# Decoder step: cache loads under the projection, eight gate chunks in each attention stage, the causal triangle as a product

## What is computed

```
u = rmsnorm(x) * g_mix
z = u @ w_in          # q, k, v of 12 dilated heads; q, k, v of 8 stick-breaking heads; gates ga, gb (1024 each)
x += (sigmoid(ga) * (oa @ w_oa) + sigmoid(gb) * (ob @ w_ob)) @ w_out
```

```
log_1mb = where(j < i, -softplus(s), 0);  suffix = cumsum from the right
a = where(j < i, exp(-softplus(-s) + suffix - log_1mb), 0);  ob = a @ v
```

## Time and profile before

| | |
|---|---|
| Time, median of 3 runs | 2026.39 us (2022.48 to 2026.89) |
| Profiled execution, its own time | 2021.45 us |
| Span of its trace | 2019.8 us |
| TensorE busy | 1746.6 us (86%) |
| VectorE busy | 1197.1 us (59%) |
| ScalarE busy | 962.2 us (48%) |
| Mean DMA rate | 186 GB/s |

### The profile page before, as it was taken

One profiled execution on the slowest core, in us unless ns is written; L12 is line 12 of the kernel. 1 busy time (PEld: TensorE's weight loads), 2 busy tenths in 40 slices (PEclk: granted clock), 3 DMA queues, 4 the chain that ended last, 5 costly groups with the idle time before them and its releaser, 6 DMA issues. The chain is left out here.

```text
span 2019.8 us, 27422 instructions
## 1 busy us (share of the span) xinstructions
PE 1746.6 (86%) x9832; PEld 1491.5 (74%) x9832; DVE 1197.1 (59%) x1564; ACT 962.2 (48%) x1351; POOL 200.5 (10%) x294
## 2 busy tenths in 40 slices
PE   5999999959888887676597973999999999994898
PEld 4999999948666666354496852788888888873785
DVE  5122221125499997432464236899999999993664
ACT  4112111111476775134442112778787878782454
POOL 0011110030000000000130001311111111111000
PEclk7999999979899999675798985999999999997899
DMA  4344443196351200500345314999999999993420
GB/s 126 116 125 126 126 126 105 53 275 215 100 179 53 74 31 19 193 1 12 105 136 180 125 44 147 386 387 385 384 382 383 389 389 384 388 384 125 175 79 32
DMA packets 151862, 375.80 MB, mean 186 GB/s; under 512 B 21507, under 2 KB 94835, under 8 KB 131300
## 3 DMA queue, kind: packets, MB, share of 16 engines
q1 hardware_dynamic: 116594, 308.16, 42.2%
q0 software_dynamic: 15424, 36.00, 5.7%
q10 hardware_dynamic: 19762, 30.56, 4.4%
HBM read 326.86 MB, written 72.12 MB: 198 GB/s over the span
## 5 line engine op out<-in xcount | busy, mean ns | idle before, releaser
L96 PE MATMUL p_acc<-uh,p_wl 128*128 128x344 f32 x720 | 234.9, 326 | 8.5 <-DVE ul L329 8.5
L98 PE MATMUL p_acc<-uh,p_wh 128*128 128x344 f32 x720 | 231.1, 321 | 0.0
L97 PE MATMUL p_acc<-ul,p_wh 128*128 128x344 f32 x720 | 231.1, 321 | 0.0
L306 ACT ACTIVATE p_zc<-p_acc 128x344 f32<-128x344 f32 x90 | 41.2, 457 | 292.4 <-PE p_acc L98 288.1
L2313 DVE TENSOR_TENSOR x_wgl<-x_wg,x_wgh 128x2048 fp32r<-128x2048 f32 x66 | 148.3, 2287 | 16.2 <-ACT x_wgh L2250 14.8
L2313 DVE TENSOR_TENSOR x_wul<-x_wu,x_wuh 128x2048 fp32r<-128x2048 f32 x66 | 148.3, 2288 | 15.9 <-ACT x_wuh L2250 15.8
L2335 DVE TENSOR_TENSOR x_wdl<-u,x_wdh 128x1024 fp32r<-128x1024 f32 x128 | 148.2, 1219 | 11.2 <-ACT x_wdh L2256 11.2
L96 PEld LDWEIGHTS p_acc<-uh,p_wl 128*128 128x128 f32 x720 | 136.0, 189 | 11.9 <-issue 8.2
L342 DVE COPY p_zk<-p_tp 128x512 f32<-128x512 f32 x40 | 25.8, 686 | 193.8 <-PE p_tp L259 193.8
L97 PEld LDWEIGHTS p_acc<-ul,p_wh 128*128 128x128 f32 x720 | 136.2, 189 | 0.0
L98 PEld LDWEIGHTS p_acc<-uh,p_wh 128*128 128x128 f32 x720 | 136.2, 189 | 0.0
(11 more groups left out here) (375 smaller groups left out, 4246.7 us busy)
## 6 DMA issues: line engine op xcount, KB each, us to landing
x_wg<-in_w_gate SPq DMA_DIRECT2D x64, 1024.0 KB, 8.1
x_wu<-in_w_up SPq DMA_DIRECT2D x64, 1024.0 KB, 8.3
u<-in_w_down SPq DMA_DIRECT2D x32, 2048.0 KB, 12.6
zT<-p_zc ACTq DMA_DIRECT2D x30, 516.0 KB, 3.5
p_w<-in_w_in SPq DMA_DIRECT2D x30, 512.0 KB, 5.4
ztok<-p_zk POOLq DMA_DIRECT2D x20, 512.0 KB, 4.7
m_gate<-gT SPq DMA_DIRECT2D x16, 516.0 KB, 4.3
f_y<-ys POOLq DMA_DIRECT2D x16, 512.0 KB, 5.1
```

The source lines that it names most:

```text
L96: pe.matmul(out, w_low, m_high, start=first, stop=False)
L97: pe.matmul(out, w_high, m_low, start=False, stop=False)
L98: return pe.matmul(out, w_high, m_high, start=False, stop=last)
L306: act.activation(zc[:, b, s * NS:(s + 1) * NS], acc[b * NSPLIT + s][:, 0:NS], ACT.Copy).then_inc(zc_full, 1)
```

## The change

Three things are done together.

A class `Ahead` holds the buffers and loads of decode. `project` now issues them from SP between its passes: the window rows of keys and values, the page table, the key pages, then queries, and after the last weights the first two gate chunks. The memsets of K, Q and V move to GpSimd at the start of `project`. The passes are reordered: the five of q first and not kept, the ten of k and v last and kept. Decode itself loads only the own rows of k and v, the value pages and the stick-breaking queries. The key pages now lie where `u` was, and the by-token copies of `project` lie in a spare part of another buffer.

`DECODE_GATES` goes from 6 to 8: decode has 24 groups, stick-breaking 576 gate matmuls in place of 720. The steps of decode move forward.

The triangle is rounded once by ScalarE, and TensorE adds it to the scores of the diagonal block by a product with the identity in rounded fp32. The addition of line 678 is gone.

```diff
-DECODE_GATES = 6
+DECODE_GATES = 8
 # project
-        RUNS = [(0, CA, CA, True), (CA, KEPT, 3 * CA + CB - 2 * CA, True),
-                (KEPT, KEPT + CA // 2, -2 * KEPT, False),
-                (KEPT + CA // 2, PASSES, 3 * CA - 2 * (KEPT + CA // 2), False)]
+        RUNS = [(0, CA // 2, 0, False), (CA // 2, QUERIES, 2 * CA, False),
+                (QUERIES, QUERIES + CA, -CB, True), (QUERIES + CA, PASSES, 0, True)]
...
+            def ahead(n):
+                if n == 0:
+                    a.cached(sp, a.K, 0, 0, a.kq_in)
+                    a.cached(sp, a.V, 1, 0, a.v_in)
+                if n == 1:
+                    sp.wait_ge(cleared, 3)
+                    for x in (1, 2):
+                        a.cached(sp, a.K, 0, x, a.kq_in)
+                        a.cached(sp, a.V, 1, x, a.v_in)
+                    sp.dma_start(a.table[:, :], ...)
+                if n == 2:
+                    sp.wait_ge(ul_full, KD)
+                    sp.wait_ge(a.table_in, 16)
+                    for b in range(DEC // 2):
+                        a.load_page(sp, a.PK, b, 0, a.ek_in[b])
+                if n == 3:
+                    for b in range(DEC // 2, DEC):
+                        a.load_page(sp, a.PK, b, 0, a.ek_in[b])
+                    for b in range(2):
+                        sp.wait_ge(k_out[b], QUERIES * 16)
+                    for x in range(N_DIL):
+                        a.query(sp, x, a.kq_in)
+                        a.own_row(sp, a.Q, 0, x, a.kq_in)
+            each_pass(sp, step, ahead)      # ahead(n) follows the first pass of run n
+            for c in range(2):
+                sp.dma_start(a.gw[c], win_v[:, :, QKV + c * P:QKV + (c + 1) * P]).then_inc(a.gw_in[c], 16)
 # decode_and_gates
-        D_SCORES_T, D_PROBS_T, D_VALUES = 6, 7, 8
-        S_SCORES_T, S_WEIGHTS_T, S_VALUES = 13, 14, 16
-        S_SCORES = {8: (0, 2), 9: (2, 4), 10: (4, 6), 11: (6, 8)}
+        D_SCORES_T, D_PROBS_T, D_VALUES = 4, 5, 6
+        S_SCORES_T, S_WEIGHTS_T, S_VALUES = 10, 11, 13
+        S_SCORES = {4: (0, 2), 5: (2, 4), 6: (4, 6), 7: (6, 8)}
...
-                if n == D_SCORES_T - 3:
+                if n == 0:
                     dilated_scores(0)
                     dilated_scores(1)
 # stick_and_gates, TensorE
+                edge = c * HALF + n == (i + 1) * P
                 for b in range(2):
-                    pe.matmul(S[:, b, 0:n], q..., k..., start=True, stop=True).then_inc(s_full, 1)
+                    last = pe.matmul(S[:, b, 0:n], q..., k..., start=True, stop=not edge, ...)
+                    if edge:
+                        last = pe.matmul(S[:, b, n - P:n], unit_r[:, :], causal[:, :], start=False, stop=True, ...)
+                    last.then_inc(s_full, 1)
 # ScalarE
+            act.activation(unit_r[:, :], ident[:, :], ACT.Copy).then_inc(rounded, 1)
+            act.wait_ge(const, 2)
+            act.activation(causal[:, :], drawn[:, :], ACT.Copy).then_inc(rounded, 1)
 # VectorE
-                    diag = z[:, u % ZB, i * P:(i + 1) * P]
-                    dve.tensor_tensor(diag, diag, causal[:, :], ALU.add).then_inc(masked, 1)
...
-                    dve.wait_ge(masked, u + 1)
+                    dve.wait_ge(z_full, scaled(u) + 1)
```

More of the change, by code:

```diff
@@ L210, in project @@
             "p_uh_full", "p_ul_full"))
+        cleared = sem("p_cleared")
+        a = g["ahead"]
         u, uh, ul, ident, zT, ztok = g["u"], g["uh"], g["ul"], g["ident"], g["zT"], g["ztok"]
@@ L215, in project, with each_pass @@
         PASSES = CHUNKS // 2
-        KEPT = CA + CB
+        QUERIES = (CA + CB) // 2
+        KEPT = PASSES - QUERIES
         GROUPS = [(0, 4), (4, 4)]
-        RUNS = [(0, CA, CA, True), (CA, KEPT, 3 * CA + CB - 2 * CA, True),
-                (KEPT, KEPT + CA // 2, -2 * KEPT, False),
-                (KEPT + CA // 2, PASSES, 3 * CA - 2 * (KEPT + CA // 2), False)]
-        def each_pass(eng, step):
-            for lo, hi, shift, kept in RUNS:
+        RUNS = [(0, CA // 2, 0, False), (CA // 2, QUERIES, 2 * CA, False),
+                (QUERIES, QUERIES + CA, -CB, True), (QUERIES + CA, PASSES, 0, True)]
+        def each_pass(eng, step, between=None):
+            for n, (lo, hi, shift, kept) in enumerate(RUNS):
                 step(lo, shift, kept)
+                if between:
+                    between(n)
                 inner = hi - (hi == PASSES)
@@ L237, in final, with opens @@
             return isinstance(it, int) and it == PASSES - 1
-        def kept_before(it):
-            return isinstance(it, int) and it <= KEPT
+        def opens(it):
+            return isinstance(it, int) and it == QUERIES
         @block.sync
@@ L281, in step @@
                     elif not first(it):
-                        turn(it - 1, 1, kept or kept_before(it))
+                        turn(it - 1, 1, kept and not opens(it))
             each_pass(pe, step)
-            turn(PASSES - 1, 1, False)
+            turn(PASSES - 1, 1, True)
         @block.scalar
@@ L349, in _ @@
         def _(pool):
+            for t in (a.K, a.Q, a.V):
+                pool.memset(t[:, 1, :, :], 0.0).then_inc(cleared, 1)
             def step(it, shift, kept):
@@ L546, in scores @@
                     need(pe, z_full, z_first[st, c] - 1 + b)
-                    pe.matmul(S[:, b, 0:n], q[x][h, i * P:(i + 1) * P], k[x][h, c * HALF:c * HALF + n],
-                              start=True, stop=True).then_inc(s_full, 1)
+                    last = pe.matmul(S[:, b, 0:n], q[x][h, i * P:(i + 1) * P], k[x][h, c * HALF:c * HALF + n],
+                                     start=True, stop=not edge, skip_group_check=True)
+                    if edge:
+                        last = pe.matmul(S[:, b, n - P:n], unit_r[:, :], causal[:, :], start=False, stop=True,
+                                         skip_group_check=True)
+                    last.then_inc(s_full, 1)
             def turn(u):
@@ L1178, in decode_and_gates @@
                 "e_sT_full", "e_z_full", "e_w_full", "e_t_full", "e_al_full", "e_a_full", "e_aT_full",
                 "e_aT_read", "e_oT_full"))
-        ek_in = [sem(f"e_k_in{b}") for b in range(DEC)]
-        gw_in = [sem(f"g_w_in{j}") for j in range(2)]
+        kq_in, v_in, ek_in, gw_in = a.kq_in, a.v_in, a.ek_in, a.gw_in
         g_out = [sem(f"g_g_out{j}") for j in range(2)]
         gwh_full, gwl_full, acc_full, gate_full = map(sem, ("g_wh_full", "g_wl_full", "g_acc_full", "g_gate_full"))
-        pages = g["cache_sb"].rearrange("a n k c h d -> (a n) k c (h d)")
@@ L1233, in _ @@
+            for x in range(N_DIL):
+                a.own_row(sp, K, A_W, x, kq_in)
             for x in range(N_DIL):
[L1234 to L1237 removed]
+                a.own_row(sp, V, 2 * A_W, x, v_in)
             sp.wait_ge(scored, 2)
             for b in range(DEC):
[L1240 to L1241 removed]
+                a.load_page(sp, PV, b, 1, ev_in)
@@ L2719, in build @@
             g["spare_small"] = flat2[:, (CB + 4) * NT:TT * D]
-            before = list(nc.free_semaphores)
-            with nc.sbuf_tensor("u", [P, KD, NT], F32) as g["u"]:
+            opened = ExitStack()
+            ahead_sem = lambda n: ctx.enter_context(nc.semaphore(n))
+            with nc.sbuf_tensor("s_bias0", [P, 2], F32) as bias0, nc.sbuf_tensor("u", [P, KD, NT], F32) as g["u"]:
+                g["ahead"] = Ahead(g, lambda n, s, d=F32: opened.enter_context(nc.sbuf_tensor(n, s, d)), ahead_sem)
+                before = list(nc.free_semaphores)
                 norm_in(nc, g, x_of)
                 project(nc, g)
-            with nc.sbuf_tensor("e_pk", [P, 8 * SEQ], F32) as shared, nc.sbuf_tensor("s_bias0", [P, 2], F32) as bias0:
+                shared = g["u"][:, :, :].rearrange("p k n -> p (k n)")[:, 0:8 * SEQ]
                 part = [shared[:, n * SEQ:(n + 1) * SEQ] for n in range(8)]
```

147 lines of the change are left out of this document (66 added, 81 removed).

## The result

The changed kernel took 2029.09 us, the median of 10 runs (2027.33 to 2034.82), beside 2025.15 (2021.01 to 2027.45) for the kernel before on the same chip: a ratio of 1.0030, 95% interval 1.0018 to 1.0042 (here and below the ratio is estimated over all the runs together; the two medians alone give 1.0019). It is slower by 0.2 to 0.3%. The forecast was 2018.0, faster by 0.4%. The profiled execution's span grew from 2019.8 to 2027.2 us.

The account below looks back on a forecast made before the run. TensorE was taken to bound the projection, loads to cost decode about 13 us, and VectorE to pace stick-breaking. Projection +3.7, decode +6.9 and stick-breaking −19 gave −8.4 us: median 2018.0, range 2008 to 2029.

Parts of the forecast that it names:

- Stick-breaking: the mask: Stick-breaking: VectorE loses 64 additions, −12.8 us, and waits, −1.6; TensorE's 64 added products, 8.3 us, fit its waiting.
- Projection: Projection: the added loads cost TensorE 0 us, bounds 0 and +5.
- End of the projection: Last projection pass, now a kept one: added transposes, copies and stores end the block 3.7 us later, bounds +2 and +6.
- Start of decode: Decode before ScalarE's first cut: gate weights already loaded, so three of four issues and a wait go, −2.4 us.
- The new one before the dilated outputs: Decode step 8: TensorE waits for VectorE's d_own, a new stall of 2.5 us, bounds 0 and 6.
- Two chunks fewer in stick-breaking: Stick-breaking: less gate work gives −2.3 us for VectorE's cuts, −2.9 in the opening, −1.5 in the drain.
- The opening's −2.9: Stick-breaking's opening: the third cut moves to step 4, so the first scan starts earlier, −2.9 us.
- A, the clock: Stick-breaking: TensorE's clock falls in more places, 2 us each; slower from six on, 2034 with eight; chance 0.11.
- three signs that I named as disproof: TensorE waits in projection; stick-breaking's granted clock below 0.95; VectorE's waits for transposes from 6.4 to over 15 us.
- B, the loads: Projection: load bursts delay weights and stall TensorE, +9 us, so 2027; chance 0.05 at twice its price.
- C: Stick-breaking gives only mask and cuts, −14 us, decode's new stall is 6; net 0, 2026; chance 0.22 with other small forms.
- D: All waits go: no new decode stall, projection's end costs 2, stick-breaking gives 25; −18.6 us, 2008; chance 0.19.

Follow-up runs that it names:

- grouped order: The changed kernel with both heads' score products issued first and both triangle products after them; 2016.59 us, ratio 0.9968.
- the pair was split: The kernel before, with one gate product per step from step 8 on moved between both heads' score products, no mask on TensorE; 2032.46 us, ratio 1.0044.

## Why the prediction was wrong

The ratios split the change as the sum did, each times 2022 us. In the sum, loads are +3.7 − 2.4 − 12.9 − 1.2 − 1.7 + 2.5 = −12.0; the two chunks are +22.6 − 2.3 − 2.9 − 1.5 = +15.9; the mask is −12.8 − 1.6 + 0.7 + 1.4 = −12.3.

| part | forecast | measured | from |
|---|---|---|---|
| loads and steps | −12.0 | −11.5 | 0.9943 − 1 |
| two chunks to decode | +15.9 | +19.8 | 1.0041 − 0.9943 |
| mask on TensorE | −12.3 | −2.2 | 1.0030 − 1.0041 |
| sum | −8.4 | +6.1 | 1.0030 − 1 |

The −2.2 of the mask is smaller than the intervals of the two ratios are wide (5 and 6 us), so it can't be told from nothing.

*The step that failed* is in "Stick-breaking: the mask": "I take 0.129, 8.3 us; all of it lies inside TensorE's 39.4 us of waiting for VectorE, and nothing is added." I priced 64 products by their own length and said of their place only that a change of kind might treble it. What counted was what stood on either side: two products that had shared the engine. TensorE's work grew by 34.5 us instead, and the stage came out 1.1 us longer and not 19 shorter. The upper bound, 25 us, was also under the 34.5, because it was a bound on the masks and not on their neighbours. The trace of before showed both heads' 384 keys as one group of four records, 0.85 us, but no head alone to hold it against; the shape in that row, 64*128, and the slices of 64 partitions in the code were what could have made me ask. The Trainium skill ("TensorE: Matmul & The Clock Gate", "The mechanism") says that small products on different row groups of the array overlap, and that a weight load overlaps a running product only where the row groups differ. On the first the traces agree (0.85 us for two heads, 0.84 for one). On the second they don't as it stands: in the projection products and weight loads take all 128 rows, and TensorE is busy 240.00 and its loads 239.19 of the same 240 us. That a product over all rows between the two heads ends their overlap is shown; by what mechanism is not.

With the order mended, the kernel has a ratio of 0.9968; the forecast was 2018.0 / 2026.39 = 0.9959. That they are so near is partly luck: the stage is then 10.1 us shorter, where 19 was forecast. The mask in the grouped order takes 6.4 off it and not 12.3, and what follows the last gate eviction happened to be 3.8 shorter in that profile.

*The terms, one by one.* Projection: right, 240.00 of 240, no wait for weights. End of the projection: +1.9, not +3.7, just under my lower bound of 2. Start of decode: from first issue to first cut 1.74 us (411.73 to 413.47) in place of 4.05, so −2.3, near the −2.4 of the forecast. The stall of 12.9 went. The new one before the dilated outputs is 1.3, not 2.5, yet it costs more than its length: the group around it takes 7.8 us (451.21 to 459.01) and not 3.77, with the clock granted at 0.76 and 0.82 of full, so for part of each at the level of 1.2 and not 2.4 GHz. I had counted a fall behind the old stall and none behind the new. Decode in all: its last eviction is 11.0 later, the sum to that point was +3.7 + 6.9 = +10.6. Two errors cancel in this: the start was 1.8 us better than forecast, and decode from its first issue to its last eviction grew by 9.1 and not by 6.9.

*Two chunks fewer in stick-breaking.* The opening's −2.9 was wrong. I moved the third cut to step 4 by slower filling; it stays in front of the first scan, behind a longer wait than before (7.43):

```profile
551.07 1.23 DVE L762 TENSOR_TENSOR s_g_wl<-u,s_g_wh 128x1024 fp32r<-128x1024 f32 x1 [9.80 <-ACT s_g_wh L705]
552.21 2.29 DVE L774 TENSOR_TENSOR_SCAN s_w<-s_w,u 128x1024 f32<-128x1024 f32 x1
```

The first line is the cut, the second the scan. The scan starts about 12 later, with decode ending 11.0 later. Nor does it gain where only the two chunks differ: the first scan starts 13.2 after the first z with six chunks in decode and 13.4 with eight. The stage is 6.8 shorter between these two, near −2.3 − 2.9 − 1.5 = −6.7, so the size was right and the place of the −2.9 was not. The whole price of the two chunks, 19.8, is 3.9 above the forecast; between the two kernels that differ in them alone the stages' marks account for 15.0 (+21.8 and −6.8), and where the rest lies, beyond the variation of what follows, stays open.

*The rivals.* A, the clock: the granted clock in stick-breaking is 0.96, down from 0.98, but it is not what decides. The kernel with the grouped order has 0.95 there and is the faster, the one with the lost pairing in the kernel before has 0.99. Of the three signs that I named as disproof, the waits for transposes spoke clearly, 19.9 against a limit of 15; the clock stands at the limit, 0.96 in this window and 0.94 from decode's last eviction on. B, the loads: refuted, and it was the least likely. C was nearest in size, for another reason: its stick-breaking still gave 14 us, and the measured one gave nothing. D was the case in which no wait is left in decode; one was left. None of my cases had TensorE's work grow by more than the masks' own length; "work that leaves TensorE there gives little back" was right, and I took it for its reverse, that work added there costs little.

## What to carry to other kernels

Before putting an operation between two others, ask whether these two run at the same time: on TensorE, products of 64 rows from different halves, which the timeline merges into one group, are the case to look for. Price work that is added to an engine with free time by what is left of that free time, with the neighbours' loss in it, and expect a part to leak out (11 of 37 us where the pair was split, with TensorE then at 96%) before the engine is quite full. When one part of a change pays for another, measure them apart: two chunks moved to decode gave away more than the loads had earned.

## What the runs showed of the hardware

Two fp32 products of 64 rows each, on different halves of TensorE's rows, take the time of one: 0.85 us against 0.84 at 384 columns, 0.63 against 0.62 at 256. A 128-row product between them, a mask or a gate product, ends that; the gate product itself takes 0.36 us (621.04 to 621.40) where the pitch of such a product is 0.157. A product of 64 rows between them, on the half of the one it follows, does not end it. And some 9.9 MB of loads beside a TensorE that is never idle cost that engine nothing: the DMA engines stand at 0.47 in place of 0.44 from 61 to 301 us and, with the moved stores, at 0.45 in place of 0.24 after that, and TensorE is busy 240.00 of 240 and 101.00 of 101 us. A wait of TensorE of 1.3 us, with the granted clock at 0.85 and 0.73 in the 8 us at and behind it, cost 3 to 4 (grouped order, six chunks, with and without the wait).
